# Encoder block on 8 cores: the mean of squares of RMS norm as one f32 matmul, and another spread of the weight casts

## The reference

```
qa, ka, va, qb, kb, vb, ga, gb = split(x @ w_in)
qa, ka = rope(rms_norm(qa)), rope(rms_norm(ka))      # 8 query heads, 2 key heads of 128
out_a  = softmax(qa ka^T) va                          # all 4096 keys
out_b  = dilated window attention(qb, kb, vb)         # 3 groups of 4 heads
mixed  = (sigmoid(ga) * (out_a @ w_proj_a) + sigmoid(gb) * (out_b @ w_proj_b)) @ w_out
x = layer_norm(ALPHA * x + mixed);  x = layer_norm(ALPHA * x + swiglu(x))
rms_norm(x) = x * rsqrt(mean(square(x)) + 1e-6) * g   # over the 128 values of a head
```

## Time and profile before

| | us |
|---|---|
| three runs | 4349.01, 4854.45, 5077.53 |
| median | 4854.45 |
| profiled execution | 4337.81 |
| its span, slowest core (3) | 4335.9 |
| its other cores' spans | 4318.2 to 4331.2 |
| TensorE busy | 4069.3 (94%) |
| VectorE busy | 1643.0 (38%) |
| ScalarE busy | 1164.8 (27%) |
| GpSimd busy | 774.0 (18%) |

### The profile page before, as it was taken

One profiled execution on the slowest core, in us unless ns is written; L12 is line 12 of the kernel. 1 busy time (PEld: TensorE's weight loads), 2 busy tenths in 40 slices (PEclk: granted clock), 3 DMA queues, 4 the chain that ended last, 5 costly groups with the idle time before them and its releaser, 6 DMA issues.

```text
span 4335.9 us, 57531 instructions; the slowest of 8 cores (4318.2 to 4335.9 us)
## 1 busy us (share of the span) xinstructions
PE 4069.3 (94%) x19792; PEld 1884.9 (43%) x19792; DVE 1643.0 (38%) x2561; ACT 1164.8 (27%) x1730; POOL 774.0 (18%) x918
## 2 busy tenths in 40 slices
PE   3747999989999999999899999999999999999998
PEld 1214544434554444444344444444444444444443
DVE  2635110003566888999665511101010122210007
ACT  1423000003567888888002210000000011110000
POOL 2121110011113444111006610000001111110010
PEclk7979999999999999999999999999999999999999
DMA  9073773375996232111885774444388555553675
GB/s 144 22 108 78 113 126 76 73 129 111 207 215 166 74 89 69 52 33 35 232 234 176 212 162 74 74 75 74 63 171 174 117 116 112 113 104 57 132 145 175
DMA packets 256414, 510.81 MB, mean 118 GB/s; under 512 B 61056, under 2 KB 114432, under 8 KB 247936
## 3 DMA queue, kind: packets, MB, share of 16 engines
q0 software_dynamic: 83920, 227.61, 32.3%
q1 hardware_dynamic: 172208, 279.51, 21.9%
HBM read 583.16 MB, written 150.41 MB: 169 GB/s over the span
## 4 chain that ended last, share of the span: by engine, by line
PE 77%; DVE 7%; DMA 7%; issue 4%; ACT 3%; SPq 1%; POOL 1%; DVEq 0%; ACTq 0%; POOLq 0%
PE pbig L262 77%; DVE t L274 2%; DVE PS L274 2%; ACT PT L271 1%; DMA ob<-OST 1%; DMA xTh<-xt 1%; DMA xTo<-xt 1%; SPq L268 1%; DMA qb<-QST 1%; DVE RD L291 1%; DVE stg L282 1%; ACT hl L271 1%; DVE YL L282 1%; ACT y L271 1%; DVE STAT L303 0%
## 5 line engine op out<-in xcount | busy, mean ns | idle before, releaser
L262 PE MATMUL pbig<-xTo,wbuf 128*128 128x512 bf16 x4224 | 1063.1, 387 | 79.1 <-DMA wbuf<-w_in 40.1
L262 PEld LDWEIGHTS pbig<-xTo,wbuf 128*128 128x128 bf16 x4224 | 415.0, 99 | 555.2 <-issue 118.6
L262 PE MATMUL pbig<-X1T,WG 128*128 128x512 bf16 x2816 | 636.7, 379 | 2.5 <-DMA X1T<-x1T 2.3
L262 PE MATMUL pbig<-X1T,WU 128*128 128x512 bf16 x2816 | 636.5, 379 | 0.0
L271 ACT ACTIVATE PT<-pbig,ashift 128x1024 bf16<-128x1024 f32 x512 | 557.3, 1115 | 106.4 <-DVE PS L274 59.3
L262 PE MATMUL pbig<-WD,HT 128*128 128x512 bf16 x2464 | 534.8, 380 | 4.3 <-DMA WD<-w_ffn_down 4.3
L274 DVE TENSOR_TENSOR HT<-SGL,pbig 128x512 bf16<-128x512 f32 x176 | 120.8, 687 | 1005.9 <-PE pbig L262 999.8
L271 ACT ACTIVATE SGL<-pbig 128x512 f32<-128x512 f32 x176 | 105.1, 597 | 1333.5 <-PE pbig L262 1333.4
L262 PEld LDWEIGHTS pbig<-X1T,WG 128*128 128x128 bf16 x2816 | 275.2, 98 | 334.5 <-issue 3.1
L262 PEld LDWEIGHTS pbig<-X1T,WU 128*128 128x128 bf16 x2816 | 275.6, 98 | 332.2
L262 PEld LDWEIGHTS pbig<-WD,HT 128*128 128x128 bf16 x2464 | 241.6, 98 | 297.2 <-issue 8.4
(11 more groups left out here) (117 smaller groups left out, 3505.7 us busy)
## 6 DMA issues: line engine op xcount, KB each, us to landing
WG<-w_ffn_gate POOLq DMA_DIRECT2D x88, 512.0 KB, 7.3
WU<-w_ffn_up POOLq DMA_DIRECT2D x88, 512.0 KB, 9.2
wbuf<-w_in POOLq DMA_DIRECT2D x160, 256.0 KB, 10.6
WD<-w_ffn_down POOLq DMA_DIRECT2D x77, 512.0 KB, 7.0
sgb<-gstg SPq DMA_DIRECT2D x64, 256.0 KB, 3.0
SG<-sga SPq DMA_DIRECT2D x64, 256.0 KB, 9.0
SG<-sgb SPq DMA_DIRECT2D x64, 256.0 KB, 9.4
YY<-xs SPq DMA_DIRECT2D x16, 1024.0 KB, 8.0
```

Source lines behind the costliest of these rows:

```text
L262: return lambda e: e.matmul(out, lhsT=lhsT, rhs=rhs, start=start, stop=stop)
```

## The change

`rms_rope` squares once, in f32, and sums with one matmul whose two operands are f32, with ones scaled to 1/128 (`onesf`). GpSimd's subtraction and ScalarE's second square are gone. The root has two buffers r of its own, in the place of hl. The casts are given out as 5 for each key block j = 13 to 17 and 2 for query blocks 6 to 9 (of which 7 pieces are left), in place of 4 and 2 for blocks 6 to 11.

```diff
--- before.py
+++ after.py
@@ -359,6 +359,7 @@
 
     ident_b = ar.alloc("ident_b", [128, 128], BF16)
     ones_b = ar.alloc("ones_b", [128, 128], BF16)
+    onesf = ar.alloc("onesf", [128, 128], F32)
     bgate = ar.alloc("bgate", [128, 32], F32)
     qkg = ar.alloc("qkg", [128, 2], F32)
     epsr = ar.alloc("epsr", [128, 1], F32)
@@ -373,8 +374,8 @@
     xTo = ar.alloc("xTo", [128, 16, T], BF16)
     xTh = ar.alloc("xTh", [128, 16, T], BF16)
     wbuf = [ar.alloc("wbuf", [128, 16, 256], BF16) for _ in range(4)]
-    F32T = ("sq", "y", "hl", "t1", "t2")
-    f32t = {n: [ar.alloc(n, [128, 512], F32) if n != "hl" else ar.alloc(n, [128, 2, 512], BF16) for _ in range(2)] for n in F32T}
+    F32T = ("sq", "y", "r", "t1", "t2")
+    f32t = {n: [ar.alloc(n, [128, 512], F32) for _ in range(2)] for n in F32T}
     gstg_off = R2 + 32768
     cct = ar.alloc("cct", [128, T], F32)
     sst = ar.alloc("sst", [128, T], F32)
@@ -411,6 +412,7 @@
     s.dma("sp", DMA(bgate[:, :], bgate_d[:, :]), writes=["bgate"])
     s.dma("sp", DMA(qkg[:, :], qkg_d[:, :]), writes=["qkg"])
     s.dve(MEMSET(ones_b[:, :], 1.0), writes=["ones_b"])
+    s.dve(MEMSET(onesf[:, :], 1.0 / 128.0), writes=["onesf"])
     s.dve(MEMSET(epsr[:, :], RMS_EPS), writes=["epsr"])
     s.dve(MEMSET(epsl[:, :], LN_EPS), writes=["epsl"])
     s.dve(MEMSET(epsl4[:, :], 4.0 * LN_EPS), writes=["epsl4"])
@@ -450,14 +452,12 @@
     def rms_rope(bank, tb, gcol, scale, dst_dram, dkey):
         i = cnt["rr"] % 2
         cnt["rr"] += 1
-        sq, y, hl, t1, t2 = (f32t[n][i] for n in F32T)
+        sq, y, r, t1, t2 = (f32t[n][i] for n in F32T)
         tl = tb % 4
         cc_ = cct[:, tl * 512:(tl + 1) * 512]
         ss_ = sst[:, tl * 512:(tl + 1) * 512]
         K = lambda n: (n, i)
         s.act(ACTF(sq[:, :], psb[bank][:, :], AF.Square), reads=[PSK(bank)], writes=[K("sq")])
-        s.act(ACTF(hl[:, 0, :], psb[bank][:, :], AF.Square), reads=[PSK(bank)], writes=[K("hl")])
-        s.pool(TT(hl[:, 1, :], sq[:, :], hl[:, 0, :], ALU.subtract), reads=[K("sq"), K("hl")], writes=[K("hl")])
         s.act(ACTF(y[:, :], psb[bank][:, :], AF.Copy, scale=qkg[:, gcol:gcol + 1]), reads=[PSK(bank), "qkg"], writes=[K("y")])
 
         s.dve(TT(t1[:, :], y[:, :], cc_, ALU.mult), reads=[K("y"), ("cc", tl)], writes=[K("t1")])
@@ -467,16 +467,13 @@
 
         def stage_b():
             pa = 4 + i
-            r = sq
-            for e2 in range(2):
-                s.pe(MM(psb[pa][:, :], ones_b[:, :], hl[:, e2, :], start=(e2 == 0), stop=(e2 == 1)),
-                     reads=[K("hl"), "ones_b"], writes=[PSK(pa)])
-            s.act(ACTF(r[:, :], psb[pa][:, :], AF.Ln, bias=epsr[:, 0:1], scale=1.0 / 128.0), reads=[PSK(pa), "epsr"], writes=[K("sq")])
-            s.act(ACTF(r[:, :], r[:, :], AF.Exp, scale=-0.5), reads=[K("sq")], writes=[K("sq")])
+            s.pe(MM(psb[pa][:, :], onesf[:, :], sq[:, :]), reads=[K("sq"), "onesf"], writes=[PSK(pa)])
+            s.act(ACTF(r[:, :], psb[pa][:, :], AF.Ln, bias=epsr[:, 0:1], scale=1.0), reads=[PSK(pa), "epsr"], writes=[K("r")])
+            s.act(ACTF(r[:, :], r[:, :], AF.Exp, scale=-0.5), reads=[K("r")], writes=[K("r")])
             si = cnt["stg"] % 4
             cnt["stg"] += 1
-            s.dve(STT(stg[si][:, :], t1[:, :], scale, sq[:, :], ALU.mult, ALU.mult),
-                  reads=[K("t1"), K("sq")], writes=[("stg", si)])
+            s.dve(STT(stg[si][:, :], t1[:, :], scale, r[:, :], ALU.mult, ALU.mult),
+                  reads=[K("t1"), K("r")], writes=[("stg", si)])
             s.dma("sp", DMA(dst_dram, stg[si][:, :]), reads=[("stg", si)], writes=[dkey])
 
         rr_pending.append(stage_b)
@@ -679,7 +676,7 @@
         elif j % 2 == 0:
             load_w(order[ji + 2])
             load_w(order[ji + 3])
-        precast(4 if 13 <= j < 18 else (2 if j < 12 else 0))
+        precast(5 if 13 <= j < 18 else (2 if j < 10 else 0))
         if j < 12:
             for cc in range(2):
                 qb_head(sj, cc, (j - 6) * 2 + cc)
```

## The result

| | before | changed |
|---|---|---|
| all runs, us | 4349.01, 4854.45, 5077.53, 4358.90 | 4180.28, 4835.84, 4459.85, 4182.03 |
| median of all | 4606.67 | 4320.94 |
| profiled execution | 4337.81 | 4180.28 |
| its span, slowest core | 4335.9 | 4178.4 |
| value block of mixer A starts, by core | 392.7 to 399.0 | 244.8 to 248.4 |

The ratio of the changed kernel's time to that of the kernel before is 0.9603, 95% interval 0.9555 to 0.9651: faster by 4.0%. A second set of runs gave 0.9597 (0.9555 to 0.9639).

A forecast was written before the change was run, and what follows sets the result against it. Before the value block, the square's ring held heads at 5.9 us and GpSimd's queue stalled TensorE and loads. 4337.8 less 157.1 (62 shorter heads, 95 stalls) and 2 for casts gives 4178.7, said as 4180; range 4150 to 4240.

The forecast's parts named there:

- The level: Whole run: 4337.8 us profiled less the savings gives 4180, range 4150 to 4240, for executions like the profiled one.
- The ring: Heads before the value block: the square stops waiting for VectorE's stg; 5.91 to 4.32 us a head, 62 us over 39.
- The f32 sum: TensorE, each head: one f32 matmul replaces two bf16 ones and costs 0.86 us, between 0.43 and 1.6.
- Four uncovered weight loads: TensorE, f32 sum: if four loads stayed uncovered, a head would take 4.75 us, 17 us more over 39 heads.
- The queue: GpSimd's queue before the value block: without subtractions loads issue early and no load is waited for; two stalls, 95 us.
- One sign: GpSimd's load issues: x blocks 4 and 5 would be issued before 100 us.
- The casts: First query block gains 6 us of its 12.19 us wait, key blocks lose 4; together -2 us.
- The dearer sum: TensorE's f32 sum costs 1.6 us, 29 us more in all: 4208, or 4220 with bad casts; chance 0.15.
- the other ring: ScalarE's Ln, waiting for the f32 sum, keeps heads at 5.9 us; only queue stalls go: 4242; chance 0.05.
- the late load: x blocks 4 and 5 meet other traffic or weight block 4 stays late: 4190 to 4220; chance 0.08.
- The slower one: The f32 matmul in all 48 heads eats the gain, at 4.9 us a sum; 2% slower needs 7.2; chance 0.02.

The follow-up runs named there:

- own_r_only: The kernel before with two buffers of its own for the root and nothing else; 4269.05 us profiled, ratio 0.985.
- sum_twice: The changed kernel with each f32 sum issued twice; 4231.01 us profiled, ratio 0.969 to the kernel before.
- casts_only: The kernel before with the new spread of casts alone; 4336.59 us profiled, ratio 0.9996.
- late_x: The changed kernel with a GpSimd memset delaying the issues of x blocks 4 to 7 and weight block 4; 4226.91 us profiled, ratio 0.9749 to the kernel before.

## Why the prediction was right or wrong

**The level was wrong, by a step that the prediction names and passes over.** It says that "the forecast is made for executions like the profiled one", though of the three times shown two were 500 us and more above that. The median of the changed kernel's four runs, 4320.94, lies outside 4150 to 4240, since two of them are executions with a lower clock on one die; the others, 4180.28 and 4182.03, are within 2.1 us of the 4180 forecast. Either kernel has such executions, the changed one in 6 of 12, at 4277 to 4938 us. The failed step is thus the last, from a difference to a time: the sum puts at nothing the 500 us by which the median of the times before stood above the profiled execution. The difference held (0.9603, where 4180 / 4337.8 is 0.9636); the median of four did not follow from one profiled execution. Why a die's clock is lower in some executions stays open; no run here tells it.

**The ring: right.** 4.32 us a head forecast, 4.31 measured; 39 x 1.6 = 62 us. VectorE's first product lost its 0.4 us. own_r_only adds what the prediction did not see: with the subtraction left beside it, VectorE bounds the head at 4.7 us.

**The f32 sum: right in size.** 0.86 us taken, between ends of 0.43 and 1.6; 0.86 measured, twice over (start to start in the changed kernel, and 33.7 / 39 in sum_twice). By the four passes of the Trainium skill (FP8 and Floating Point Precision, TensorE Precision Notes), an estimate at 0.216 us a pass is 0.86 too, and the trace agrees. Four uncovered weight loads, the prediction's other estimate from the Trainium skill, don't show: the sum has two load records of 0.193 us each, longer than the 0.107 of that estimate, but beside other matmuls, and the head did not grow to 4.75.

**The queue: right, one term mis-sized.** Weight block 4, x6 and x7 came before their heads. The ninth head's products ended at 75.5, not 70.1, since the last quarter of x block 1 took 23.47 us to land in place of 18.44. Those 5.4 us are most of the difference between 241.1 forecast and 247.2 measured for the value block. The forecast copied a landing time from a trace in which TensorE, ScalarE and the stores of the heads stood still at that moment; in the changed kernel 76 matmuls run from 50 to 69 us, over four heads, and heads are stored beside them. It is no chance of one core: the load of x block 1 that stands in the chain of waits took 18.2 to 20.3 us to land on the 24 cores of before, casts_only and own_r_only, where TensorE stands, and 20.4 to 24.4 on 57 cores of eight profiles in which heads run on (22.2 to 24.2 on the 8 of the changed kernel's). From 50 to 69 us the queue of the loads moved 3.21 MB before and 2.71 MB in the changed kernel, where SP's queue moved another 0.62 MB. An estimate from that, 18.44 x 3.21 / 2.71 = 21.8 us, gives the stores about two thirds of the delay. No run takes the stores away alone, so this is argued and not shown. One sign was missed by a little: the last issue of x blocks 4 and 5 came at 103.38 us, not before 100.

**The casts: right in kind, one part mis-sized.** The first query block lost all 12.2 us, not 6; the key blocks cost 3.2 us, not 4. Sum 9.0 in place of 2. Together 151.0 + 9.0 = 160.0, where 159.1 was forecast and 157.5 measured between the two profiled executions: errors of 6 and 7 us cancelled, and 2.5 us are not accounted for. That 4180 was met to 2 us is in this part luck.

**The rivals.** The dearer sum, the other ring and the late load are each excluded by their rows (0.86, 4.31, no wait for a weight block over 0.2 us). The slower one would have needed a sum of 4.9 us.

## What to carry to other kernels

An operation on a queue that also issues loads has two prices. It waits behind the issues ahead of it: 34.65 us before the first sum. And the loads behind it wait for it, which shows not at the operation but at the start of the next stage: 40.10 us here, 35.7 by late_x. Together the two were 81 to 89 of the 151 us. When the in-order queue of one engine issues the loads, look at what stands before each issue. And where the times of one kernel lie 15% and more apart, a difference worked out from one profiled execution forecasts the ratio and not the median of a few times.

## What the hardware showed that was not expected

- A VectorE operation with two SBUF inputs that starts beside a GpSimd subtraction of 128x512 took 1.65 us in place of 0.68, the subtraction itself 1.46 on average in place of 1.15. In the kernel before it cost another operation 0.4 us. Both ended 0.54 to 0.56 us behind the end of the subtraction, so the price depends on where the two meet.
- An f32 matmul of 128x512 shows as two records and costs 0.86 us, four times the 0.216 of a bf16 one, with its weight loads (two records of 0.193 us) covered by the matmuls around it.
- With the DMA engines full, a load of 512 KB that casts to bf16 took 20.4 to 24.4 us to land where heads were computed and stored beside it (57 cores), and 18.2 to 20.3 where TensorE stood (24 cores).
